# The passage between two blocks: the context's norm in the down stage ahead of it, final norm and next norm in one, context's products in between

## The reference

```python
def first_block(x, ...):
    ...
    return rms_norm(h, final_norm)

def modulate(x, g, shift, scale):
    return rms_norm_2(x, g) * (1 + scale) + shift

def second_block(x, c, ctx, c_ctx, ...):
    for l in range(DEPTH):
        hl = modulate(x_lat, norm_g[l, 0], mod_l[0], mod_l[1])
        hc = modulate(x_ctx, norm_g[l, 0], mod_c[0], mod_c[1])
        # even layer: both are multiplied by w_in (2832 columns)
```

## Time and profile before

| | us |
|---|---|
| runs before (3): median, lowest, highest | 1961.49, 1960.19, 1961.82 |
| the profiled execution: its own time | 1962.88 |
| its span | 1961.1 |
| TensorE busy | 1822.8 (93%) |
| ScalarE, VectorE, POOL busy | 876.4, 712.7, 936.3 |

### The profile page before, as it was taken

How to read it: one execution, slowest core, us unless ns; L and a number is a source line. 1 busy time by engine, 2 the same in 40 slices (tenths; PEclk the granted TensorE clock), 3 DMA queues, 4 the chain that set the end, 5 groups by cost and what they waited for, 6 DMA issues and landing times.

```text
span 1961.1 us, 26131 instructions
## 1 busy us (share of the span) xinstructions
PE 1822.8 (93%) x10342; PEld 1471.6 (75%) x10342; DVE 712.7 (36%) x1596; ACT 876.4 (45%) x1542; POOL 936.3 (48%) x408
## 2 busy tenths in 40 slices
PE   8999999998899998989789989999999798899998
PEld 6668887776688876878445677888878676679986
DVE  3433332145333312382465434333301343344421
ACT  4655444356554434333424524444422255556653
POOL 5646666675266666342112024444434161138876
PEclk9999999999899998999775999999999899999999
DMA  7328996543189954122000022333322431136654
GB/s 259 99 97 260 306 307 232 183 131 128 50 282 306 306 205 147 61 85 81 27 1 1 1 86 71 102 93 101 96 87 97 97 108 44 44 86 172 186 166 143
DMA packets 257419, 261.38 MB, mean 133 GB/s; under 512 B 11139, under 2 KB 201827, under 8 KB 251027
## 3 DMA queue, kind: packets, MB, share of 16 engines
q1 hardware_dynamic: 257011, 259.14, 41.9%
q10 hardware_dynamic: 288, 0.59, 0.1%
HBM read 258.66 MB, written 1.05 MB: 132 GB/s over the span
## 4 chain that ended last, share of the span: by engine, by line
PE 79%; DVE 8%; ACT 5%; DMA 4%; issue 2%; POOL 1%; SPq 1%; DVEq 0%; ACTq 0%
PE bank L347 22%; PE bank L348 21%; PE bank L349 20%; PE bank L1394 2%; PE bank L731 2%; PE bank L754 2%; PE bank L1043 2%; ACT work L1161 1%; ACT weights_high L334 1%; PE bank L1013 1%; PE bank L1745 1%; DMA work<-in_ada_w 1%; DVE work L1122 1%; PE bank L739 1%; PE bank L402 1%
## 5 line engine op out<-in xcount | busy, mean ns | idle before, releaser
L341 POOL TENSOR_TENSOR weights_low<-weights,weights_high 128x1024 fp32r<-128x1024 f32 (+1 forms) x388 | 917.7, 2382 | 913.5 <-ACT weights_high L334 913.0
L334 ACT ACTIVATE weights_high<-weights 128x1024 fp32r<-128x1024 f32 (+1 forms) x388 | 401.2, 1045 | 474.1 <-PE bank L349 141.5
L347 PE MATMUL bank<-normed_features_high,weights_high 128*128 128x256 f32 (+1 forms) x1408 | 441.7, 314 | 3.9 <-DVE normed_features_low L509 2.6
L349 PE MATMUL bank<-normed_features_low,weights_high 128*128 128x256 f32 (+1 forms) x1408 | 436.2, 310 | 0.0
L348 PE MATMUL bank<-normed_features_high,weights_low 128*128 128x256 f32 (+1 forms) x1408 | 436.2, 310 | 0.0
L347 PE MATMUL bank<-weights_high,normed_features_high 128*128 128x512 f32 (+4 forms) x752 | 291.7, 388 | 21.4 <-DVE normed_features_low L509 8.4
L347 PEld LDWEIGHTS bank<-normed_features_high,weights_high 128*128 128x128 f32 x1408 | 268.7, 191 | 56.3 <-issue 36.2
L349 PEld LDWEIGHTS bank<-normed_features_low,weights_high 128*128 128x128 f32 x1408 | 268.7, 191 | 14.0
L348 PEld LDWEIGHTS bank<-normed_features_high,weights_low 128*128 128x128 f32 x1408 | 268.9, 191 | 13.6
L349 PE MATMUL bank<-weights_low,normed_features_high 128*128 128x512 f32 (+4 forms) x752 | 276.7, 368 | 0.0
L348 PE MATMUL bank<-weights_high,normed_features_low 128*128 128x512 f32 (+4 forms) x752 | 276.1, 367 | 0.0
(11 more groups left out here) (299 smaller groups left out, 2073.6 us busy)
## 6 DMA issues: line engine op xcount, KB each, us to landing
work<-in_ada_w SPq DMA_DIRECT2D x48, 1024.0 KB, 8.1
weights<-in_ffn_w_up SPq DMA_DIRECT2D x44, 1024.0 KB, 6.3
weights<-in_ffn_up SPq DMA_DIRECT2D x44, 1024.0 KB, 6.0
weights<-in_ffn_w_down SPq DMA_DIRECT2D x20, 1024.0 KB, 5.1
weights<-in_ffn_down SPq DMA_DIRECT2D x20, 1024.0 KB, 5.0
weights<-in_diff_w_qkv SPq DMA_DIRECT2D x12, 1024.0 KB, 5.0
weights<-in_hyb_w_in SPq DMA_DIRECT2D x11, 1024.0 KB, 5.2
weights<-in_odd_w_in SPq DMA_DIRECT2D x9, 1024.0 KB, 5.3
```

The source lines that it names most:

```text
L334: A.eng.activation(high(whigh[:, m % HIGHS, :]), raw(wslot[:, u % SLOTS, :]), ACT.Copy).then_inc(scalar_done, A.one(("A", "high", m)))
L341: G.eng.tensor_tensor(raw(wlow[:, u % SLOTS, :]), raw(wslot[:, u % SLOTS, :]), high(whigh[:, m % HIGHS, :]).bitcast(F32), ALU.subtract).th ...
L347: T.eng.matmul(out_, lh, rh, start=first, stop=False)
L349: return T.eng.matmul(out_, lh, rl, start=False, stop=last)
```

## The change

The context's norm moves into "1.1 ffn down": its statistics give two diagonal matrices, 16 float32 products turn and scale the context tokens in one, and VectorE and ScalarE make high and low parts in the eight blocks. The final norm is no longer applied ahead of the next one. ScalarE takes squares of the tokens and of tokens times gains; the root of the second, with EPS times the first added, scales the transposed tokens; the gains are folded into the modulation column (`tokens_a`). The half-0 transposes move ahead of feature step 18. In "2.0 in" TensorE makes the context tiles' products of the first cut with all four halves, with the other eight transposes behind the first and the spread of the roots behind the second half, and then the latent tiles' products; a half is let go only behind these. The final tokens themselves are written later, by two scalings. The second output banks of the down stage are 2 and 3. One more small load (128-element rows of `final_norm`) and eight more rows in a setup transpose bring the gains as columns.

```diff
@@ -434,17 +434,27 @@
             idle_bank = 1 if x_ph == "setup" else 2 if x_ph.endswith("down") else 0
             warm_T(T, idle_bank, 2 if x_ph == "setup" else 5)
+            spread_T(T, ph)
+            warm_T(T, idle_bank, 8)
+
+        def spread_T(T, ph):
             T.eng.wait_ge(vector_done, done("V", ph, "inverse"))
             for j in range(2):
                 i = T.eng.matmul(psum[SPREAD][:, j * P:(j + 1) * P], stat[:, 24 + j:25 + j].to_broadcast([P, P]), ident, start=True, stop=True)
             i.then_inc(tensor_done, T.one(("T", ph, "rstd")))
-            warm_T(T, idle_bank, 8)
...
-            V.eng.wait_ge(scalar_done, done("A", x_ph, "squares", 1))
-            V.eng.tensor_scalar(stat[:, 16:18], s2[:, :, 0], EPS, None, ALU.add).then_inc(vector_done, V.one(("V", ph, "first")))
+            if ph == "2.0 norm":
+                g2 = stat[:, 48:52].rearrange("p (t h) -> p t h", h=2)
+                V.eng.wait_ge(scalar_done, done("A", x_ph, "squares", 3))
+                V.eng.scalar_tensor_tensor(out=stat[:, 36:38], in0=s2[:, :, 0], scalar=EPS, in1=s2[:, :, 1], op0=ALU.add, op1=ALU.add).then_inc(vector_done, V.one())
+                V.eng.wait_ge(vector_done, V.n)
+                V.eng.scalar_tensor_tensor(out=stat[:, 16:18], in0=stat[:, 36:38], scalar=EPS, in1=g2[:, :, 0], op0=ALU.mult, op1=ALU.add).then_inc(vector_done, V.one(("V", ph, "first")))
+            else:
...
+        def final_tokens_V(V, ph):
+            V.eng.wait_ge(scalar_done, done("A", ph, "final root"))
+            V.eng.reciprocal(stat[:, 40:42], stat[:, 40:42]).then_inc(vector_done, V.one())
+            V.eng.wait_ge(vector_done, V.n)
+            for j, t in enumerate(LAT):
+                V.eng.tensor_scalar(xt[:, t, :], work[:, j * D:(j + 1) * D], stat[:, 40 + j:41 + j], None, ALU.mult).then_inc(vector_done, V.one(("V", ph, "final tokens")))
+
...
+            A.eng.wait_ge(scalar_done, done("A", x_ph, "gained" if ph == "2.0 norm" else "squares", 3))
...
+            if ph == "2.0 norm":
+                A.eng.activation(stat[:, 40:42], stat[:, 36:38], ACT.Sqrt).then_inc(scalar_done, A.one(("A", ph, "final root")))
+                ahead(A, first_half[next_ph] + HIGHS - 1)
...
+                if ph == "2.0 norm" and k == 1:
+                    ahead(A, first_half[next_ph] + HIGHS)
+                if x_ph != "setup" and ph != "2.0 norm" and k % 4 == 3:
                     ahead(A, first_half[next_ph] + HIGHS - 1 + k // 4)
...
+        context_k = lambda k: psum[(2, 3, 5, 6)[k % 4]][:, k // 4 * SEQ:k // 4 * SEQ + SEQ]
+        context_diag = lambda j: spread[:, SEQ + j * P:SEQ + (j + 1) * P]
...
+        def context_stats_V(V):
+            s2 = stat[:, 0:4].rearrange("p (t h) -> p t h", h=2)
+            V.eng.scalar_tensor_tensor(out=stat[:, 36:38], in0=s2[:, :, 0], scalar=EPS, in1=s2[:, :, 1], op0=ALU.add, op1=ALU.add).then_inc(vector_done, V.one())
+            V.eng.wait_ge(vector_done, V.n)
+            V.eng.reciprocal(stat[:, 36:38], stat[:, 36:38]).then_inc(vector_done, V.one(("V", "context", "inverse")))
...
+        def context_diag_V(V):
+            V.eng.wait_ge(scalar_done, done("A", "context", "root"))
+            for j in range(2):
+                V.eng.tensor_scalar(context_diag(j), ident, stat[:, 40 + j:41 + j], None, ALU.mult).then_inc(vector_done, V.one())
...
+        def context_turn_T(T):
+            T.eng.wait_ge(vector_done, done("V", "context", "diag"))
+            for k in range(KT):
+                for j in range(2):
+                    i = T.eng.matmul(context_k(k)[:, j * P:(j + 1) * P], xt[:, j, k * P:(k + 1) * P], context_diag(j), start=True, stop=True)
+            i.then_inc(tensor_done, T.one(("T", "context", "turned")))
...
+        def context_V(V, which):
+            V.eng.wait_ge(tensor_done, done("T", "context", "turned"))
+            for k in range(KT + 1):
+                if k < KT:
+                    a, b = which(k, 0)
+                    V.eng.tensor_scalar(context_k(k), context_k(k), a, b, ALU.mult, ALU.add).then_inc(vector_done, V.one(("V", "context", "features", k)))
+                if k >= 1:
+                    q = k - 1
+                    V.eng.wait_ge(scalar_done, done("A", "context", "high", q))
+                    V.eng.tensor_tensor(nTl[:, q, span(CTX)], context_k(q), nTh[:, q, span(CTX)].bitcast(F32), ALU.subtract).then_inc(vector_done, V.one(("V", "context", "low", q)))
...
+        def context_A(A, k):
+            A.eng.wait_ge(vector_done, done("V", "context", "features", k))
+            A.eng.activation(nTh[:, k, span(CTX)], context_k(k), ACT.Copy).then_inc(scalar_done, A.one(("A", "context", "high", k)))
...
+        def first_cut_T(T, ph, normed, x_ph, cuts, pieces):
+
+            a, b = cuts[0]
+            taken, done_ = [], {}
+            T.eng.wait_ge(vector_done, done("V", "context", "low", KT - 1))
+            for tiles in (CTX, LAT):
+                for h4 in range(4):
+                    if tiles is CTX:
+                        taken.append(take_half(T))
+                    wh, wl, m = taken[h4]
+                    for p in pieces:
+                        if p["c"] != 0 or p["t"] not in tiles:
...
+                        if h4 == 0 and tiles is LAT:
+                            T.eng.wait_ge(vector_done, done("V", normed, "features", 0))
+                        for kk in range(2):
+                            k = 2 * h4 + kk
+                            if tiles is LAT:
+                                T.eng.wait_ge(vector_done, done("V", normed, "low", k))
+                            tok = slice(p["t"] * P, (p["t"] + 1) * P)
+                            i = product(T, psum[p["n"]][:, 0:b - a], (nTh[:, k, tok], nTl[:, k, tok]), (wh[:, kk, :], wl[:, kk, :]), k == 0, k == KT - 1)
+                        if p["j"] == 3:
+                            half_read(T, i, m)
...
+                    if tiles is CTX and h4 == 0:
+                        turn_x_T(T, normed, x_ph, 1)
+                    if tiles is CTX and h4 == 1:
+                        spread_T(T, normed)
...
+        DOWN_BANKS = {"1.0 ffn down": (7, 4, 0, 1), "1.1 ffn down": (7, 4, 2, 3), "2.0 ffn down": (4, 5, 6, 7, 0, 1, 2, 3), "2.1 ffn down": (0, 1, 6, 7)}
...
+                    if ph == "1.1 ffn down" and half == 0 and f0 == 6:
+                        context_turn_T(T)
+                    if ph == "1.1 ffn down" and half == 1 and f0 == 0:
+                        T.eng.wait_ge(vector_done, done("V", "context", "low", KT - 1))
...
+        gained = lambda j, c: work[:, j * D + 512 * c:j * D + 512 * c + 512]
+
+        def gained_tokens_V(V, ph, c):
+            V.eng.wait_ge(vector_done, V.n)
+            for j, t in enumerate(LAT):
+                V.eng.tensor_tensor(gained(j, c), xt[:, t, 512 * c:512 * c + 512], final_g[:, 512 * c:512 * c + 512], ALU.mult).then_inc(vector_done, V.one(("V", ph, "gained", 2 * c + j)))
...
+        def last_down_A(A, ph, parts):
+            A.eng.wait_ge(scalar_done, A.n)
+            A.eng.activation(stat[:, 32:33], const("ident", 0, 1), ACT.Sqrt).then_inc(scalar_done, A.one())
+            context_root_A(A)
+            for c in range(2):
+                for m in range(FC // 2):
+                    ahead(A, first_half[ph] + FC // 2 * c + m + 1 + HIGHS - (2 if c == 1 and m >= FC // 2 - 2 else 0))
+                    if c == 0 and 3 <= m < 7:
+                        context_A(A, 2 * m - 6)
+                        context_A(A, 2 * m - 5)
+                squares_A(A, ph, [(("V", ph, "x", n), bank, t, a, b) for n, (_, bank, t, a, b) in enumerate(parts)][2 * c:2 * c + 2])
+                for j in range(2):
+                    A.eng.wait_ge(vector_done, done("V", ph, "gained", 2 * c + j))
+                    A.eng.wait_ge(scalar_done, A.n)
+                    A.eng.activation(psum[parts[2 * c + j][1]][:, :], gained(j, c), ACT.Square, scale=D ** -0.5,
+                                     accum_out=stat[:, 48 + 2 * j + c:49 + 2 * j + c]).then_inc(scalar_done, A.one(("A", ph, "gained", 2 * c + j)))
+
...
+            if layer == 0:
+                tokens_a = acol[:, 0:16].rearrange("p (k s) -> p k s", s=2)[:, :, 1]
+                V.eng.wait_ge(vector_done, V.n)
+                V.eng.tensor_tensor(tokens_a, tokens_a, veccol[:, 80:88], ALU.mult).then_inc(vector_done, V.one())
...
-            T.eng.transpose(psum[5][:, 0:80], vrows, const("ident", 0, 80, slice(0, 80)))
+            T.eng.transpose(psum[5][:, 0:88], vrows, const("ident", 0, 88, slice(0, 88)))
...
-            phase(ph, lambda T: (norm_T(T, nm, tiles), proj_T(T, ph, cuts, pieces, banks, between, nm)),
-                  lambda V: (norm_V(V, nm, tiles), norm_evac_V(V, nm, tiles, which), proj_read(V, ph, cuts, pieces, banks, dst, after_V)),
-                  lambda A: (norm_A(A, nm, tiles), norm_evac_A(A, nm, tiles), proj_read(A, ph, cuts, pieces, banks, dst, after_A)))
+            x_ph = "1.1 ffn down"
```

(24 more changed lines are left out.)

44 lines of the change are left out of this document (28 added, 16 removed).

## The result

The changed kernel takes 1952.0 us (median of 7 runs, 1943.24 to 1955.18); the kernel before, run beside it, 1960.19 (7 runs, 1957.99 to 1964.76). The ratio is 0.9945, with a 95% interval of 0.993 to 0.996: faster by 0.4 to 0.7%. That is inside the predicted range and on the predicted side, but of 13.7 us forecast as won, 8.2 arrived (1960.19 - 1952.0). The executions don't lie evenly: three of the seven at 1943.24 to 1945.85, four at 1952.0 to 1955.18. The profiled execution took 1952.65, its span is 1950.8, so the profile shows 10.3 us won (1961.1 - 1950.8).

What follows compares the result with a forecast made beforehand. TensorE, busy 93%, bounds the kernel, so only its idle or low-clock time can be won. Before 40.25 us; after 5.1 (down stage) + 21.5 (passage) = 26.6; gain 13.7 from 1961.5 gives 1947.8 us, range 1944.5 to 1952.2.

Steps and rivals of the forecast that it cites:

- Item 1: Down stage, TensorE: the context's turn with the diagonal, 16 float32 products; adds 3.8 us, bounds 1.8 to 6.1.
- Item 2: Down stage, TensorE: eight early transposes ahead of feature step 18 of half 1; adds 0.9 us, bounds 0.8 to 1.5.
- Item 3: Down stage: TensorE's new wait for the diagonal; 0 us, bounds 0 to 1.3.
- Item 4: Down stage: context blocks on VectorE, about 0.9 us each, less on ScalarE; covered, adds nothing; without cover 7.2 us.
- Item 5: Down stage, half 0: VectorE's products of tokens and gains contend with POOL; 0.4 us reaches TensorE, bounds 0 to 2.4.
- The passage: From E, the end of the last down product, to the second cut: 40.25 us before, 21.5 after the change.
- the third rival: Passage: better overlap, no stop for weight halves 2 and 3, 18.8 us in all; time 1945.1; chance 0.10.
- clock fall in the gaps: Passage: TensorE's clock falls in the two gaps of 1.7 and 1.0 us, costing 3 us; time 1950.8; chance 0.13.
- wait at half 1: Down stage, start of half 1: a late weight transfer holds context blocks and TensorE; slower, time 1966.8; chance 0.03.
- The gate chain moved along: Behind the second cut: rival that the gain is waited for again at VectorE's gate chain; time 1961.5; chance 0.02.
- Behind 812.59 all engines are shifted alike: From the second cut's first product on: later stages only move earlier, and the wait for the gate chain stays.
- signs of being wrong: Clock falls behind E; second cut later than E + 25; down stage grows over 7 us; gate-chain wait grows by the gain.

Runs made afterwards that it cites:

- early_halves: Changed kernel with ScalarE copying weight halves 2 and 3 before the squares of tokens times gains, and the spread one half later; median 1938.69 us.
- context_alone: Changed kernel with only the context's part: final and next norm stay apart, gains not folded, no early transposes; median 1948.36 us.
- after_again: The changed kernel run once more, unedited; median 1953.27 us, ratio to the kernel before 0.9955 to 0.9979.
- early_shift: early_halves plus nine dummy float32 products (2.0 us) on TensorE ahead of the second cut; median 1951.07 us.
- gate_warm: Changed kernel plus 36 dummy float32 products ahead of TensorE's wait for the gate chain before L1851; median 1956.57 us over 12 runs.

## Why the prediction was right, and where it wasn't

**The down stage** was forecast to grow by 5.1 us and grew by 4.6. Item 1, the turn: 3.8 forecast, 3.58 measured (717.75 - 714.27, plus 0.10 that the next product takes longer); two records for each float32 product, at the warming products' spacing, as assumed. Item 2: 0.9 and 0.80. Item 3: no wait, as said, with 1.6 us to spare; the two small products took 2.70, one POOL operation in their way. Item 4: covered as said. Item 5: 0.4 forecast, 0.07 measured (TensorE's stop is 0.54 against 0.47), though the mechanism is there: the pair of token products takes 2.35 beside a running POOL and 1.29 beside an idle one. The Trainium skill's rule (SBUF — State Buffer, Who interferes with whom) agrees with that row; what was held was mostly VectorE, which had time.

**The passage**: 21.43 against 21.5. The spread starts at E + 5.2 (forecast 5.3), the stop for half 2 is 1.76 (1.7), that for half 3 is 0.50 (1.0), the clock is 1.00 throughout. early_halves shows that ScalarE's order of work made the two stops, as the forecast's list has it; without them the passage takes 19.40, where the third rival has 18.8.

**The rivals**: no clock fall in the gaps of the changed kernel, but context_alone shows that a gap of the same 1.8 us can bring one. No wait at half 1. The gate chain moved along: TensorE's wait of 9.21 us stays.

**The step that failed** is "Behind 812.59 all engines are shifted alike". The instructions are, but not their durations: the stretch to the gate products took 309.0 instead of 302.9 us at a lower mean clock. The prediction looked for the clock inside the passage alone and took the 112.6 us at 1.2 GHz behind it for fixed. They are not: over fourteen profiled executions that stretch takes between 293.9 and 319.0 us, and medians move by up to 12 us for a 2 us shift. Of the prediction's signs of being wrong only the gate chain's wait lies there, so none could show it. With the local 14.39 and a stretch as before, the profiled execution would have had a span of about 1945 instead of 1950.8. The forecast of -13.7 was right for the edit and 5.5 too good for the medians (8.2), and the range held because other terms had made it wide, not because this one was in it. That it held is luck besides: 1952.0 is 0.2 under its upper end, 1952.2; after_again's median, 1953.27, lies beyond; and the kernel before ran 1.3 us faster beside the changed one (1960.19) than the forecast had it (1961.49). In the range itself one sum is off: item 1's lower end gives 1945.8 (1947.8 - 2.0), not 1944.5, which changes nothing here.

## What to carry to other kernels

Count a change in two places: at the next fixed point behind it, and at the end; if they differ, compare the granted clock of the stages between before looking for a new wait. Where a profile shows tens of microseconds of TensorE at the lower clock, a range of a few microseconds for a shift ahead of it is too narrow, and a result of that size says little about the edit: delay the same kernel by a known 2 us, look at all its executions and not at the median alone, and compare stretches in which the clock falls at the same distance behind a fixed point. Filling the longest idle wait with dummy products, placed so that nobody waits for them, was worth here about as much as the edit, in the one kernel in which it was tried.

## What the runs showed of the hardware

A later start of 2.0 us made a kernel 9 us faster (1952 to 1953 against 1943.35) and another 12 us slower (1938.69 against 1951.07), by the clock of stages 50 to 300 us behind the delay: in the first case the profiles show it (0.84 against 0.80 over the stretch), in the second the mean clock of whole executions (0.950 to 0.952 in the four of early_shift at 1949 and above, 0.953 to 0.960 in early_halves).

A TensorE that the profile calls busy is not one that keeps its clock: in the window 1040 to 1060 of the changed kernel it is busy for 20.00 of 20 us, with weight loads for 8.54, at a granted 0.50. The passage, busy for 19.18 of 21.44 with weight loads for 18.60, keeps 1.00 through stops of 1.76 and 0.50.

Profiled executions of different kernels in which the clock falls at the same place behind the second cut (49.1 to 49.4 us) need the same 302.67 to 302.88 us for the stretch behind it, with 112.6 us of it at the lower clock.

In an idle wait of 9.21 us the clock went from 1.00 to 0.50 and stayed low for 13.7 us; with dummy products in the wait it stayed up through it and was then low for 6.8 us, and the later low stretches took less time too (85.3 us in all instead of 122.9). The Trainium skill (TensorE: Matmul & The Clock Gate, What's actually happening) says that the clock follows how busy the array has been, and that the chip's watch runs on its own and does not start over with a kernel, so that the place of a change varies from run to run. The two groups of gate_warm's runs agree; no run here shows what the watch counts.
